# Reciprocal roots with one Newton step and one cubic step in an encoder kernel on Trainium2

## The chip, the cores and the metric

The kernel runs on one core of a Trainium2 chip. Five engines work side by side and wait for one another by semaphores: TensorE (in the profile PE, its weight loads PEld), VectorE (DVE), ScalarE (ACT), GpSimd (POOL) and SyncE (SP), which issues the transfers. The metric is the time of one execution on the device in microseconds.

## The reference

Two transformer blocks of different make stand behind one another. Norms are everywhere in them, and each needs the reciprocal of a square root:

```python
def rms_norm(x, gain=None):
    xf = x.astype(jnp.float32)
    y = xf * lax.rsqrt(jnp.mean(xf * xf, axis=-1, keepdims=True) + EPS)   # EPS = 1e-6
    ...
def _layernorm(x, g, b):
    ...
    y = (xf - mu) * lax.rsqrt(var + LN_EPS) * g.astype(jnp.float32) + b.astype(jnp.float32)
```

In the first block (two layers, on 256 rows of x and 256 rows of the context z, 1024 wide), each of

```python
x = x + 0.5 * mx[2] * swiglu(modulate(rms_norm(x), mx[0], mx[1]), ffn1_w1[l], ffn1_w3[l], ffn1_w2[l])
hx = modulate(rms_norm(x), mx[3], mx[4]) @ w_in[l]
x = x + mx[5] * (mix_x @ w_out[l])
x = x + 0.5 * mx[8] * swiglu(modulate(rms_norm(x), mx[6], mx[7]), ffn2_w1[l], ffn2_w3[l], ffn2_w2[l])
```

has a norm over a row; the heads of the attention branches and of the gated linear attention are normed one by one. The second block (two layers) norms its latents, the heads of a difference attention, and its rows by layer norms.

## The kernel before

TensorE multiplies in float32 by three products (high x high, low x high, high x low; lines L119 to L121). The weights come as chunks of 1 MB in a ring of buffers; ScalarE copies a chunk to its high half (L266, in the second block L2172), VectorE subtracts to get the low half (L277, L2180). The chunks are worked in one long order, and the stages between projections (norms, turns, attention) are woven into it step by step: an engine takes a step of a stage at set places between the groups of its products, so each engine has one fixed queue, and what stands ahead in it delays what follows. Products with the unit matrix (`stream`, L127) fill set numbers of places at which TensorE would wait.

A row norm with its turn is the stage `RmsTurn`. ScalarE squares the rows in four halves and sums each half (L1054 in `Residual`, L1091 in `Squares`) into `row_squares`; VectorE adds the two halves (L1221), applies the mean's factor 1/1024 and epsilon (L1222), takes the reciprocal root (`root_steps`), and writes it on two diagonal matrices (L1225), with which TensorE turns and scales the rows (L1197, 32 rows in the trace). ScalarE and VectorE then apply the modulation (L1142, L1160) and split the result (L1151, L1168). There are 11 such stages.

`root_steps` is used by all norms: for a row norm on a tile 128 x 2, for the norms of heads on 128 x 4 to 128 x 16 (`HeadNorm`, L1762; GpSimd multiplies by its result, L1773), for the latents (`Norms`, L2545), for the heads of the difference branch (`DiffNorm`, L2729; the product L2734 follows) and for the layer norms (`LayerNorm`, L2912; L2918 and ScalarE's L2886 follow). It makes a first guess from the bits (L1239 shifts, L1240 subtracts from a constant) and takes three Newton steps, r <- r (1.5 - 0.5 s r^2), of three operations each (L1242 to L1244). All are on VectorE and each waits for the one before by a semaphore (`link`).

In the profile further names stand: L733 turns the modulation's columns out of PSUM and so frees a bank for L711, the modulation's products; L830 multiplies the gate of a feed-forward network and frees a bank too; L781 makes the low half of that product, for which the next down projection waits in `DownPiece.pe` before its first group and before any step that is woven into it; L2493 finds an attention row's maximum for ScalarE's exponential L2471.

Of the kernel before, what the change touches and what calls it, by code (L numbers as in the profile page):

```python
# [11 lines left out]
ACT = mybir.ActivationFunctionType  # L12
ALU = mybir.AluOpType
# [3 lines left out]
D = 1024  # L17
# [23 lines left out]
EPS = 1e-6  # L41
# [69 lines left out]


ROOT_GUESS = float(0x5F3759DF)
TAB = dict(le=0, gt=1, lt=2, ge=3, ones=4)


# [79 lines left out]
class Woven:  # L196
# [59 lines left out]
    def hi(self, act, m, h, own=False):  # L256

        if m >= len(self.pieces):
            self.follow.hi(act, m - len(self.pieces), h)
            return  # L260
        if not self.pieces[m].parted or (self.pieces[m] in self.own_hi and not own):
            return
        s, r = m % RING, self.half(m, h)
        if h == 0:
            act.wait_ge(self.loaded[s].sem, self.loaded[s].at(m // RING + 1))
        act.activation(self.high[s][:, r], self.raw[s][:, r], ACT.Copy).then_inc(self.highs.sem, 1)  # L266

    def lo(self, dve, m, h, own=False):

        if m >= len(self.pieces):  # L270
            self.follow.lo(dve, m - len(self.pieces), h)
            return
        if not self.pieces[m].parted or (self.pieces[m] in self.own_lo and not own):
            return
        s, r = m % RING, self.half(m, h)
        dve.wait_ge(self.highs.sem, 2 * self.pieces[m].parted_before + h + 1)
        dve.tensor_tensor(self.low[s][:, r], self.raw[s][:, r], self.high[s][:, r].bitcast(F32),  # L277
                          ALU.subtract).then_inc(self.lows.sem, 1)
# [5 lines left out]
    def lo_next(self, dve, m, h):  # L284

        if not self.over_raw(m + 1):
            self.lo(dve, m + 1, h)
# [56 lines left out]
class Piece:  # L344
# [24 lines left out]
    def act(self, act, step):  # L369
        n = self.steps  # L370
        for s in range(n // 2):
            step()
        self.early("act", act)
        self.w.hi(act, self.m + 2, 0)
        for s in range(n // 2, n):
            step()
        self.w.hi(act, self.m + 2, 1)
        self.late("act", act)

    def dve(self, dve, step):  # L380
        n = self.steps
        self.w.lo_next(dve, self.m, 0)
        for s in range(n // 4):
            step()
        self.w.lo_next(dve, self.m, 1)
        for s in range(n // 4, n // 2):
            step()
        self.early("dve", dve)
        for s in range(n // 2, n):
            step()  # L390
        self.w.lo_ahead(dve, self.m)
        self.late("dve", dve)
# [24 lines left out]
class After(Stage):  # L417
# [11 lines left out]
    def pe(self, pe):  # L429
        yield from self.hold("pe")  # L430
# [586 lines left out]
class Residual(Stage):  # L1017
# [32 lines left out]
    def act(self, act):  # L1050
        for b in range(4 if self.ss is not None else 0):
            t, side = b // 2, slice((b % 2) * 512, (b % 2 + 1) * 512)
            act.wait_ge(self.added.sem, self.added.at(b + 1))
            last = act.activation(self.w.ps[:, b, :], self.x[:, t, side], ACT.Square, accum_out=self.ss[:, t, b % 2:b % 2 + 1])  # L1054
        if self.ss is not None:
            last.then_inc(self.squares.sem, 1)
        yield


class Squares(Stage):  # L1060
# [24 lines left out]
    def act(self, act):  # L1085
        self.ready(act)
        if self.side:
            act.wait_ge(self.opened.sem, self.opened.at(1))
        for b in range(4):
            t, side = b // 2, slice((b % 2) * 512, (b % 2 + 1) * 512)  # L1090
            last = act.activation(self.w.ps[:, 4 + b % 2 if self.side else b, :], self.x[:, t, side], ACT.Square,  # L1091
                                  accum_out=self.ss[:, t, b % 2:b % 2 + 1])
            if b < 3:
                self.w.act_link(last)
        last.then_inc(self.squares.sem, 1)
        yield
# [77 lines left out]
class RmsTurn(AffineTurn):  # L1174
# [43 lines left out]
    def dve(self, dve):  # L1218
        b, link = self.b, self.w.dve_link
        self.squares(dve)  # L1220
        link(dve.tensor_tensor(b["var"][:, :], self.ss[:, :, 0], self.ss[:, :, 1], ALU.add))  # L1221
        link(dve.tensor_scalar(b["var"][:, :], b["var"][:, :], 1.0 / D, EPS, ALU.mult, ALU.add))  # L1222
        root_steps(dve, link, b["var"][:, :], b["root"][:, :], b["root_tmp"][:, :])
        for t in range(2):
            dve.tensor_scalar(b["diag"][:, t, :], self.w.eye, b["root"][:, t:t + 1], None, ALU.mult).then_inc(self.scaled.sem, 1)  # L1225
        yield
        yield from [False] * self.lag
        yield from self.held("dve")
        for part in range(2):
            self.mod.wait_part(dve, self.part + part)  # L1230
        if self.room:
            self.room(dve)
        self.dve_turn(dve)
        yield


def root_steps(dve, link, ss, r, t, done=None):

    link(dve.tensor_scalar(t.bitcast(I32), ss.bitcast(I32), 1, None, ALU.arith_shift_right))  # L1239
    link(dve.tensor_scalar(r.bitcast(I32), t.bitcast(I32), -1.0, ROOT_GUESS, ALU.mult, ALU.add))  # L1240
    for i in range(3):
        link(dve.tensor_tensor(t, r, r, ALU.mult))  # L1242
        link(dve.scalar_tensor_tensor(out=t, in0=t, scalar=-0.5, in1=ss, op0=ALU.mult, op1=ALU.mult))
        last = dve.scalar_tensor_tensor(out=r, in0=t, scalar=1.5, in1=r, op0=ALU.add, op1=ALU.mult)  # L1244
        if i < 2 or done is None:
            link(last)
        else:
            last.then_inc(done.sem, 1)


class OutPiece(ProjectionPiece):
# [240 lines left out]
class GlaLevels(Stage):  # L1492
# [29 lines left out]
    def pe(self, pe):  # L1522
        w, f, a, dec = self.w, TAB, self.a, self.dec
        self.ready(pe)
        for kind, m, pair in self.order:
            if kind == "decay":
                w.open(pe, 4)
                for d in range(2):
                    for t in range(2):
                        tab = len(TAB) + d * GLA_LEVELS + m if m < GLA_LEVELS else ((f["gt"], f["le"]), (f["ge"], f["lt"]))[d][t]  # L1530
                        at = (2 * d + t) * P
# [78 lines left out]
class GlaState(Stage):  # L1610
# [13 lines left out]
    def pe(self, pe):  # L1624
        w, f = self.w, TAB
        parts = [[[(0, f["gt"]), (1, f["ones"])], [(1, f["gt"])]], [[(0, f["lt"])], [(1, f["lt"]), (0, f["ones"])]]]
# [88 lines left out]
class HeadNorm(Stage):  # L1715
# [36 lines left out]
    def dve(self, dve):  # L1752
        link, n = self.w.dve_link, self.n
        flat = [self.s[k][:, 0:2 * n] for k in ("ss", "root", "tmp")]
        ss = flat[0].rearrange("p (t h) -> p t h", t=2)
        dve.wait_ge(self.squares.sem, self.squares.at(1))
        for t in range(2):
            last = dve.tensor_reduce(ss[:, t, :], self.junk[:, t, 0:n * HD].rearrange("p (h d) -> p h d", d=HD), AX, ALU.add)
        last.then_inc(self.summed.sem, 1)
        dve.wait_ge(self.summed.sem, self.summed.at(1))  # L1760
        yield
        link(dve.tensor_scalar(flat[0], flat[0], 1.0 / HD, EPS, ALU.mult, ALU.add))  # L1762
        root_steps(dve, link, *flat, done=self.roots)
        yield
# [755 lines left out]
class Norms:  # L2520
# [21 lines left out]
    def dve(self, dve):  # L2542
        m, link = self.mla, self.w.dve_link
        dve.wait_ge(self.squares.sem, self.squares.at(1))
        link(dve.tensor_scalar(m["ss"][:, 0, :], m["ss"][:, 0, :], 1.0 / Q_LORA, EPS, ALU.mult, ALU.add))  # L2545
        link(dve.tensor_scalar(m["ss"][:, 1, :], m["ss"][:, 1, :], 1.0 / KV_LORA, EPS, ALU.mult, ALU.add))
        flat = lambda a: a[:, :, :].rearrange("p a t -> p (a t)")
        root_steps(dve, link, flat(m["ss"]), flat(m["root"]), flat(m["root_tmp"]))
        dve.tensor_copy(m["ss"][:, 0, 0:1], m["root"][:, 0, 0:1]).then_inc(self.roots.sem, 1)
        yield  # L2550
# [1623 lines left out]
```

## Time and profile before

| | us |
|---|---|
| median of 3 runs | 3108.55 |
| lowest, highest | 3102.3, 3112.1 |
| profiled execution | 3110.55 |
| its span, first to last instruction | 3108.8 |
| TensorE busy | 3005.6 (97%) |
| VectorE busy | 1759.8 (57%), 2646 instructions |
| ScalarE busy | 1470.3 (47%), 2182 instructions |
| GpSimd busy | 152.0 (5%) |
| mean granted clock of TensorE | 0.99 of full |

A busy share says how much an engine had to do, not whether anything waited for it. For that there is the chain that ended last, followed back from the last instruction, and for each instruction the time that its engine stood still before it, with what ended that. A timeline merges instructions of one line that follow each other; the "x" is then their number and the duration that of all.

### The profile page before, as it was taken

To read this page: it belongs to the slowest core of one execution; us is meant where nothing else is said; L and a number is where in the kernel's file an instruction comes from. 1 tells how busy PE (TensorE), PEld (TensorE's weight loads), DVE (VectorE), ACT (ScalarE), POOL (GpSimd) and SP (SyncE) were. 2 spreads that over 40 slices of the span, in tenths; PEclk is the share of its full clock that TensorE was granted. 3 is DMA by queue.
4 is the path that set the end of the run, shared out by engine and by line. 5 is a ranking of instruction groups with operands and counts; after the bars stand their busy time and mean duration, and the time that the engine had idled before them with its cause. 6 is when DMAs were issued, how large, how long until landed. Compare 5 with 4: busy or idle time off the path is not lost.

```text
span 3108.8 us, 53689 instructions
## 1 busy us (share of the span) xinstructions
PE 3005.6 (97%) x23104; PEld 2756.7 (89%) x23104; DVE 1759.8 (57%) x2646; ACT 1470.3 (47%) x2182; POOL 152.0 (5%) x147
## 2 busy tenths in 40 slices
PE   8999999999999999999999999999999999999998
PEld 6899788898889998899898889999999999999997
DVE  5445555655546545455646454464756656475665
ACT  4344445453544443444444444455654444565443
POOL 0000000001000000000200000001110101110000
PEclk9999999999999999999999999999999999999999
DMA  7775445664555556765365445554355655445563
GB/s 284 276 236 165 150 163 191 209 197 137 158 192 175 185 186 203 261 217 165 122 181 165 160 157 185 189 177 135 121 161 190 202 190 154 128 122 171 172 198 132
DMA packets 409688, 556.64 MB, mean 179 GB/s; under 512 B 25276, under 2 KB 357996, under 8 KB 409068
## 3 DMA queue, kind: packets, MB, share of 16 engines
q1 hardware_dynamic: 409452, 553.20, 54.5%
q8 instruction: 183, 3.00, 0.4%
q14 instruction: 53, 0.43, 0.0%
HBM read 552.12 MB, written 1.05 MB: 178 GB/s over the span
## 4 chain that ended last, share of the span: by engine, by line
PE 85%; DVE 7%; ACT 3%; DMA 3%; issue 2%; SPq 0%; POOL 0%; DVEq 0%; ACTq 0%
PE psum L119 24%; PE psum L121 24%; PE psum L120 24%; PE psum L711 1%; DMA wr<-in_ffn_w_dram 1%; PE psum L2430 1%; DVE wl L277 1%; PE psum L1922 1%; PE psum L2346 1%; PE psum L2421 1%; DVE wl L2180 1%; PE psum L1545 1%; PE psum L1197 1%; PE psum L1532 1%; PE psum L127 1%
## 5 line engine op out<-in xcount | busy, mean ns | idle before, releaser
L277 DVE TENSOR_TENSOR wl<-wr,wh 128x1024 fp32r<-128x1024 f32 (+1 forms) x558 | 658.9, 1216 | 229.0 <-ACT wh L266 228.2
L266 ACT ACTIVATE wh<-wr 128x1024 fp32r<-128x1024 f32 (+1 forms) x558 | 554.9, 1039 | 231.0 <-DMA wr<-in_ffn_w_dram 208.7
L119 PE MATMUL psum<-xt_hi,wh 128*128 128x256 f32 (+1 forms) x2000 | 566.3, 283 | 3.5 <-DVE wl L277 2.4
L120 PE MATMUL psum<-xt_lo,wh 128*128 128x256 f32 (+1 forms) x2000 | 558.8, 279 | 0.0
L121 PE MATMUL psum<-xt_hi,wl 128*128 128x256 f32 (+1 forms) x2000 | 558.6, 279 | 0.0
L2180 DVE TENSOR_TENSOR wl<-wr,wh 128x1024 fp32r<-128x1024 f32 (+3 forms) x336 | 391.2, 1200 | 121.8 <-ACT wh L2172 120.9
L119 PEld LDWEIGHTS psum<-xt_hi,wh 128*128 128x128 f32 (+1 forms) x2000 | 377.1, 189 | 15.1 <-issue 7.5
L120 PEld LDWEIGHTS psum<-xt_lo,wh 128*128 128x128 f32 (+1 forms) x2000 | 377.2, 189 | 2.3
L121 PEld LDWEIGHTS psum<-xt_hi,wl 128*128 128x128 f32 (+1 forms) x2000 | 378.2, 189 | 0.1
L2172 ACT ACTIVATE wh<-wr 128x1024 fp32r<-128x1024 f32 (+3 forms) x336 | 323.3, 999 | 102.3 <-DMA wr<-in_mlp_w_dram 73.8
L119 PE MATMUL psum<-wh,xt_hi 128*128 128x256 f32 (+1 forms) x1280 | 366.2, 286 | 2.3 <-ACT vv L3337 1.7
L120 PE MATMUL psum<-wl,xt_hi 128*128 128x256 f32 (+1 forms) x1280 | 357.9, 280 | 0.0
L121 PE MATMUL psum<-wh,xt_lo 128*128 128x256 f32 (+1 forms) x1280 | 357.8, 280 | 0.0
L119 PE MATMUL psum<-zt_hi,wh 128*128 128x256 f32 (+1 forms) x1072 | 309.0, 288 | 4.8 <-DVE wl L277 3.6
L120 PE MATMUL psum<-zt_lo,wh 128*128 128x256 f32 (+1 forms) x1072 | 299.6, 279 | 0.0
L121 PE MATMUL psum<-zt_hi,wl 128*128 128x256 f32 (+1 forms) x1072 | 299.4, 279 | 0.0
L119 PE MATMUL psum<-wh,gated_hi 128*128 128x512 f32 x616 | 251.9, 409 | 3.7 <-DVE wl L277 2.2
L119 PEld LDWEIGHTS psum<-wh,xt_hi 128*128 128x128 f32 x1280 | 242.3, 189 | 3.2 <-DVE wl L2180 2.1
L121 PE MATMUL psum<-wh,gated_lo 128*128 128x512 f32 x616 | 243.7, 396 | 0.0
L120 PE MATMUL psum<-wl,gated_hi 128*128 128x512 f32 x616 | 243.6, 395 | 0.0
L120 PEld LDWEIGHTS psum<-wl,xt_hi 128*128 128x128 f32 x1280 | 242.1, 189 | 0.1
L121 PEld LDWEIGHTS psum<-wh,xt_lo 128*128 128x128 f32 x1280 | 241.3, 189 | 0.0
(464 smaller groups left out, 5314.7 us busy)
## 6 DMA issues: line engine op xcount, KB each, us to landing
wr<-in_ffn_w_dram SPq DMA_DIRECT2D x231, 1024.0 KB, 5.4
wr<-in_w_in_dram SPq DMA_DIRECT2D x88, 1024.0 KB, 5.3
wr<-in_w_mod_dram SPq DMA_DIRECT2D x72, 1024.0 KB, 5.1
wr<-in_mlp_w_dram SPq DMA_DIRECT2D x64, 1024.0 KB, 5.2
wr<-in_w_out_dram SPq DMA_DIRECT2D x20, 1024.0 KB, 5.1
wr<-in_mem_w_kv_dram SPq DMA_DIRECT2D x8, 1024.0 KB, 5.0
wr<-in_w_branch_dram SPq DMA_DIRECT2D x16, 512.0 KB, 3.5
wr<-in_w_branch_dram SPq DMA_DIRECT2D x8, 1024.0 KB, 5.0
```

The source lines that it names most:

```text
L119: pe.matmul(out, a[0], b[0], start=first, stop=False)
L120: pe.matmul(out, a[0], b[1], start=False, stop=False)
L121: return pe.matmul(out, a[1], b[0], start=False, stop=last)
L127: pe.matmul(out, eye, eye, start=True, stop=True)
L266: act.activation(self.high[s][:, r], self.raw[s][:, r], ACT.Copy).then_inc(self.highs.sem, 1)
L277: dve.tensor_tensor(self.low[s][:, r], self.raw[s][:, r], self.high[s][:, r].bitcast(F32), ALU.subtract).then_inc(self.lows.sem, 1)
L711: last = pe.matmul(self.group_rows(j), b["silu"][:, at:at + MOD_COLS], cols[:, j], start=(k == 0), stop=(k == 1), tile_position=(0, j * MO ...
L1197: return pe.matmul(out, self.x[:, t, k * P:(k + 1) * P], self.b["diag"][:, t, :], start=True, stop=True)
L1532: last = pe.matmul(w.ps[:, 4, at:at + P], a[:, t, d * P:(d + 1) * P], dec[:, tab, :], start=True, stop=True)
L1545: last = pe.matmul(w.ps[:, 4 + i, pair * 256 + t * P:pair * 256 + (t + 1) * P], src[:, 256 + jt * P:256 + (jt + 1) * P], src[:, it * P:(it ...
L2172: act.activation(self.high[s][:, r], self.raw[s][:, r], ACT.Copy).then_inc(self.highs.sem, 1)
L2180: dve.tensor_tensor(self.low[s][:, r], self.raw[s][:, r], self.high[s][:, r].bitcast(F32), ALU.subtract).then_inc(self.lows.sem, 1)
```

## The change

Root steps: the guess stays. The first Newton step now leaves its result multiplied by 3/8; the second step is of third order: with u = s r^2 (r the unscaled value), r <- r (15 - 10 u + 3 u^2) / 8. Since r' = 3r/8 is what is stored, four operations do it: t = r'^2, t = (64/9) t s (which is u), t = (t - 10/3) t, and r = (t + 5) r'. So nine operations become seven.

Row norms: ScalarE's squares carry a scale of 1/32, so that their sums hold the factor 1/1024 of the mean, and one operation adds the two halves and epsilon, where two stood. The order of the instructions on each engine is otherwise as it was.

```diff
@@ ROOT_GUESS
 ROOT_GUESS = float(0x5F3759DF)
+CUBIC = 3 / 8
@@ Residual.act
-            last = act.activation(self.w.ps[:, b, :], self.x[:, t, side], ACT.Square, accum_out=self.ss[:, t, b % 2:b % 2 + 1])
+            last = act.activation(self.w.ps[:, b, :], self.x[:, t, side], ACT.Square, scale=D ** -0.5,
+                                  accum_out=self.ss[:, t, b % 2:b % 2 + 1])
@@ Squares.act
-            last = act.activation(self.w.ps[:, 4 + b % 2 if self.side else b, :], self.x[:, t, side], ACT.Square,
+            last = act.activation(self.w.ps[:, 4 + b % 2 if self.side else b, :], self.x[:, t, side], ACT.Square, scale=D ** -0.5,
                                   accum_out=self.ss[:, t, b % 2:b % 2 + 1])
@@ RmsTurn.dve
-        link(dve.tensor_tensor(b["var"][:, :], self.ss[:, :, 0], self.ss[:, :, 1], ALU.add))
-        link(dve.tensor_scalar(b["var"][:, :], b["var"][:, :], 1.0 / D, EPS, ALU.mult, ALU.add))
+        link(dve.scalar_tensor_tensor(out=b["var"][:, :], in0=self.ss[:, :, 0], scalar=EPS, in1=self.ss[:, :, 1], op0=ALU.add, op1=ALU.add))
@@ root_steps
-    for i in range(3):
-        link(dve.tensor_tensor(t, r, r, ALU.mult))
-        link(dve.scalar_tensor_tensor(out=t, in0=t, scalar=-0.5, in1=ss, op0=ALU.mult, op1=ALU.mult))
-        last = dve.scalar_tensor_tensor(out=r, in0=t, scalar=1.5, in1=r, op0=ALU.add, op1=ALU.mult)
-        if i < 2 or done is None:
-            link(last)
-        else:
-            last.then_inc(done.sem, 1)
+    square = lambda: link(dve.tensor_tensor(t, r, r, ALU.mult))
+    square()
+    link(dve.scalar_tensor_tensor(out=t, in0=t, scalar=-0.5 * CUBIC, in1=ss, op0=ALU.mult, op1=ALU.mult))
+    link(dve.scalar_tensor_tensor(out=r, in0=t, scalar=1.5 * CUBIC, in1=r, op0=ALU.add, op1=ALU.mult))
+    square()
+    link(dve.scalar_tensor_tensor(out=t, in0=t, scalar=CUBIC ** -2, in1=ss, op0=ALU.mult, op1=ALU.mult))
+    link(dve.scalar_tensor_tensor(out=t, in0=t, scalar=-10 / 3, in1=t, op0=ALU.add, op1=ALU.mult))
+    last = dve.scalar_tensor_tensor(out=r, in0=t, scalar=5.0, in1=r, op0=ALU.add, op1=ALU.mult)
+    if done is None:
+        link(last)
+    else:
+        last.then_inc(done.sem, 1)
```

## Rows read from the trace of the kernel before

**Rows 1.** The page's chain that ended last, share of the span by engine

```profile
PE 85%; DVE 7%; ACT 3%; DMA 3%; issue 2%; SPq 0%; POOL 0%; DVEq 0%; ACTq 0%
```

**Rows 2.** Source view, L1239: count, duration ns min/median/max, first and last start us, forms

```profile
L1239 DVE TENSOR_SCALAR row_small<-row_small x11: 169/170/172, 14.6 to 1836.5; 128x2 int32<-128x2 int32 x11
L1239 DVE TENSOR_SCALAR head_tmp<-head_ss x11: 170/173/176, 337.4 to 1754.9; 128x8 int32<-128x8 int32 x4, 128x16 int32<-128x16 int32 x3, 128x12 int32<-128x12 int32 x3, 128x4 int32<-128x4 int32 x1
L1239 DVE TENSOR_SCALAR ln_tmp<-ln_var x4: 168/169/170, 2377.0 to 3098.3; 128x2 int32<-128x2 int32 x4
L1239 DVE TENSOR_SCALAR latent_tmp<-latent_ss x2: 169/170/171, 2072.3 to 2623.4; 128x4 int32<-128x4 int32 x2
L1239 DVE TENSOR_SCALAR diff_tmp<-diff_ss x2: 175/175/175, 2240.6 to 2784.0; 128x16 int32<-128x16 int32 x2
```

**Rows 3.** VectorE's timeline, row norm at 1189: start us, us, operation, [idle before <-releaser]

```profile
1189.00 0.16 DVE L1221 TENSOR_TENSOR row_small<-row_squares 128x2 f32<-128x2 f32 x1 [0.86 <-ACT psum L1054]
...
1189.80 0.16 DVE L1242 TENSOR_TENSOR row_small<-row_small 128x2 f32<-128x2 f32 x1
...
1191.37 0.16 DVE L1244 SCALAR_TENSOR_TENSOR row_small<-row_small 128x2 f32<-128x2 f32 x1
...
1191.96 0.44 DVE L733 STREAM_TRANSPOSE mod_turned<-psum 128x256 f32<-128x256 f32 x1
```

**Rows 4.** VectorE's timeline, head norm at 337 us, the first and the ninth Newton operation

```profile
337.84 0.17 DVE L1242 TENSOR_TENSOR head_tmp<-roots_na 128x16 f32<-128x16 f32 x1
...
339.51 0.17 DVE L1244 SCALAR_TENSOR_TENSOR roots_na<-head_tmp,roots_na 128x16 f32<-128x16 f32 x1
```

**Rows 5.** TensorE's timeline, work behind a standstill, and one L711 group without

```profile
344.50 2.02 PE L127 MATMUL psum<-eye 128*128 128x128 f32 x10 [3.41 <-DVE gated L830]
...
603.24 2.50 PE L1197 MATMUL psum<-diag,x 128*128 128x128 f32 x20 [0.96 <-DVE wl L277]
...
697.46 3.78 PE L127 MATMUL psum<-eye 128*128 128x128 f32 x16 [3.10 <-DVE gated L830]
...
1187.99 1.07 PE L711 MATMUL psum<-wr,silu_cond 128*32 128x256 f32 x16
1192.55 1.94 PE L711 MATMUL psum<-wr,silu_cond 128*32 128x256 f32 x16 [3.49 <-DVE mod_turned L733]
...
1503.53 2.47 PE L127 MATMUL psum<-eye 128*128 128x128 f32 x20 [1.89 <-issue]
...
1697.96 4.22 PE L1197 MATMUL psum<-diag,x 128*128 128x128 f32 x32 [2.82 <-DVE diag L1225]
...
1759.39 0.44 PE L1430 MATMUL psum<-eye,z_gqa_kv 128*128 128x128 f32 x2 [1.15 <-POOL z_gqa_kv L1777]
...
1839.21 5.87 PE L1197 MATMUL psum<-diag,x 128*128 128x128 f32 x32 [4.88 <-DVE diag L1225]
...
2380.77 1.07 PE L2879 MATMUL psum<-eye,x 128*128 128x128 f32 x8 [0.61 <-ACT x L2886]
...
2790.98 1.16 PE L2421 MATMUL psum<-mem_k,mem_q 128*128 128x256 f32 x4 [1.47 <-ACT probs L2471]
```

**Rows 6.** The chain that ended last, at 1692 and at its end: start us, us, what

```profile
1692.30 5.30 DMA wr<-in_w_in_dram
...
3104.33 1.28 DVE x L2983
```

**Rows 7.** VectorE's timeline at 1502.74

```profile
1502.74 0.68 DVE L781 TENSOR_TENSOR gated_lo<-gated,gated_hi 128x512 fp32r<-128x512 f32 x1
```

**Rows 8.** Source views of ScalarE's L1091 and L1142, columns as in rows 2

```profile
L1091 ACT ACTIVATE psum<-x x20: 601/602/603, 9.1 to 1835.3; 128x512 f32<-128x512 f32 x20
...
L1142 ACT ACTIVATE affine<-psum,mod x44: 543/564/568, 30.3 to 1845.8; 128x256 f32<-128x256 f32 x44
```

**Rows 9.** Windows: us, busy PE, PEld, DVE, ACT, POOL, granted clock, DMA share, GB/s

```profile
1836.00:1838.00 2.00, 0.00 (x0) 0.00 (x0) 1.58 (x10) 2.00 (x4) 0.00 (x0) 0.67 1.10 349
...
1696.00:1698.00 2.00, 0.04 (x1) 0.04 (x1) 1.72 (x11) 0.38 (x1) 0.00 (x0) 1.00 1.08 358
```

## The prediction, made before the changed kernel had run

> **What bounds the kernel now.** I read the chain of waits first: which engine's work, followed back from the last instruction, has no slack. 85% of it is TensorE and 7% VectorE [rows 1]. The change touches VectorE almost alone, so it can only count where VectorE stands in that chain. Next I read the source view of the first instruction of a root, the shift. Its counts say how many roots the program takes: 11 for the row norms (width 2), 11 for the head norms, 4 for the layer norms, 2 latent and 2 of the difference branch, 30 in all [rows 2]. Then the timeline of VectorE around them: a root is a train of small operations, each of which waits for the one before it on its own engine, so it costs its start-to-start step times its length [rows 3, 4]. Last, the timeline of TensorE, for the stretches in which it stood still and what ended them [rows 5]: only roots that such a stretch waits for are worth anything.
>
> **What the change removes.** A row norm's train before its two diagonal matrices is 13 operations now (add, mean and epsilon, shift, guess, three times three) and 10 after: the pair of additions becomes one, nine Newton operations become three and four. The other 19 roots go from nine to seven operations behind the guess. Removed in all: 11 x 3 + 19 x 2 = 71 operations. The step in a row norm is (1189.80 - 1189.00) / 4 = 0.20 us for the first ones and (1191.37 - 1189.80) / 8 = 0.196 us in the Newton part [rows 3]; in a head norm of width 16 it is (339.51 - 337.84) / 8 = 0.209 us [rows 4]. So VectorE does 71 x 0.2 = 14 us less in the whole program. The new operations have forms that the train already holds (one tensor times or plus a constant, times a tensor), so I give them the same step; the one that takes the same tile on both sides, (t - 10/3) t, has no row of its own. Its bounds are a step of 0.196 us, as its neighbours have, and twice that, if the tile had to be read twice over. I take 0.196, since the squaring L1242 reads one tile on both sides already and keeps that step; the other end stands among the rivals.
>
> The Trainium skill (VectorE: DVE Perf Modes, section on the TRN2 errata) says that a small operation pays a fixed cost whatever its width, and, in its rules for kernel authors, that one should reduce the number of operations and not the semaphores between them. By it the price is per operation, as above; steps of 0.196 us at width 2 and 0.209 us at width 16 agree.
>
> **Which of the 30 roots count.** For each I followed the chain of waits through its place.
> - Row norms: 3 of 11 are in the chain, at 597, 1189 and 1836 us. TensorE stands still behind them for 0.96, 3.49 and 4.88 us [rows 5], more than the 3 x 0.196 = 0.59 us that go, so nothing else is late first. 3 x 0.59 = 1.8 us.
> - The row norm at 1695 looks like one of them (2.82 us of standing, ended by the diagonals [rows 5]) and I count it at nothing: the chain goes round it, through a weight transfer issued at 1692.30 that lands 5.30 us later, and ScalarE's copies of it, which hold back the turn that follows [rows 6]. That transfer doesn't start earlier. If the cover is gone, 0.59 us are to be had.
> - Head norms: 7 of 11. Two before 344.50 (TensorE then waits 3.41 us for a product queued behind both on VectorE), one before 697.46 (3.10 us), two before 1503.53 (1.89 us), two before 1759.39 (1.15 us, by way of GpSimd) [rows 5]. The stretch of 1.89 us is put down to nothing by the profile; I count it because it ends 0.11 us behind the subtraction L781, which stands right behind a root on VectorE and on which the down projection's first product waits [rows 7]. 7 x 2 x 0.209 = 2.9 us, each place's share below its stretch.
> - Difference branch: both of 2, through a maximum and an exponential (1.47 us before 2790.98, and a like one of 0.85 us before the other) [rows 5]. 2 x 2 x 0.209 = 0.8 us.
> - Layer norms: all 4; TensorE waits 0.61 us before 2380.77 [rows 5], 0.83 and 0.87 us at the two like places, against 0.39 us that go, and behind the last one there is only VectorE until the end [rows 6]. 4 x 2 x 0.196 = 1.6 us.
> - The other 14 (8 row, 4 head, 2 latent) stand where TensorE is busy or waits for a transfer or ScalarE. Nothing.
>
> Sum on the path: 1.8 + 2.9 + 0.8 + 1.6 = 7.1 us, half of the 14 us. The 16 roots are one behind another in one chain, so the shares add.
>
> **The squares.** The scale in the Square activations changes no count. Such an activation takes 602 ns for 512 columns [rows 8]. The nearest row for a dearer form is L1142, which takes its scale and shift from columns of a tile: 564 ns for 256 columns, where half of 602 would be 301 [rows 8]; not all of that is the operands. Were the scale to cost 0.16 us an activation, the two places where ScalarE's squares are in the chain (one before 1189, four before 1836) would give back 5 x 0.16 = 0.8 us. Lower bound 0. I take 0, since the scale here is a constant in the instruction and the compared form reads two columns. The Trainium skill (ScalarE: Activation LUTs, What ACT_TABLE_LOAD costs) says that an operand read from a column adds to an activation and a constant scale or bias doesn't; no row here shows a Square with a scale.
>
> **The sum.** The profiled execution took 3110.55 us, 1.75 us over its span; 3110.55 - 7.1 = 3103.5. It lies 2.0 us above the median of the runs, 3108.55; from that it is 3101.5. The profiled one holds four falls of the clock that I price next, and looks like one of the dearer executions; I forecast **3101.5 us**.
>
> **Rivals.** *Clock falls that go with the standing.* At 1836 to 1838 us, while TensorE stood, its granted clock went to 0.67 on the mean of 2 us, so to the lower of its two levels (1.2 of 2.4 GHz); at 1696 to 1698, after 2.82 us of standing, it stayed at 1.00 [rows 9]. What a fall costs: the same 32 diagonal products took 5.87 us behind it and 4.22 us without [rows 5], 1.65 us; the 16 products L711 at 1192.55 took 1.94 us against 1.07 us at 1187.99, as at 62 other places. The clock fell at four of the stretches above (3.41, 3.10, 3.49 and 4.88 us) and not at 2.82 or 1.89 us. The change makes these 2.6, 2.7, 2.9 and 4.3 us. If three of the four falls go, at 1.7 to 2.5 us each, another 5 to 7.5 us go: 3094 to 3096.5 us. With one or two gone it is 3097 to 3100. For: the three land at or under a length that was spared. Against: one spared stretch is no rule, and other stretches of 2 to 3 us may take their turn. The Trainium skill (TensorE: Matmul & The Clock Gate, Part 1) says that the chip judges activity on a beat of its own that doesn't start with the kernel; by it a shorter standing makes a fall less likely, without a fixed boundary, and moves it from run to run. It is a reason for a spread of a few us, such as the 3102.3 to 3112.1 of the runs before.
>
> *The gain is taken back by what is late next.* Weight transfers at 1695 already do that. If a transfer or ScalarE's copies were as late at 1189, 1836 and the two attention places (1.8 - 0.6 + 0.8 = 2.0 us) and the stretch put down to nothing isn't ended by L781 (0.8 us), 4.3 us are left: 3104.3 us. The length of the stretches speaks against it.
>
> *The change doesn't do what it says.* If the operation (t - 10/3) t took two steps, the 16 roots of the chain would give back 16 x 0.196 = 3.1 us: 3101.5 + 3.1 = 3104.6 us; with the squares' 0.8 us on top 3105.4 us. If every one of the three or four new forms did, nothing would be left. L1242's rows speak against it.
>
> *Slower.* The clock falls more often: the schedule behind 337 us shifts against the chip's beat, and stretches that were spared (2.82, 1.89, 0.96 us, those of the layer norms) come to fall. At 2.5 us a fall and 7.1 us in hand, three falls more than now bring it to nothing, and from seven more on (7 x 2.5 - 7.1 = 10.4 us) it is slower than 0.3%: about 3119 us. All but the first of the spared stretches get shorter, so this needs ill luck seven times.
>
> **How the numbers follow.** What a measurement of this kernel can tell from no change is about 0.3%, 9.3 us: the bound is 3099.2 us. Forecast case, the sum with at most one fall gone or come (3099 to 3104): 0.50, of which 0.04 below the bound. Falls go with the standing: 0.33, all below it but 0.01. Taken back: 0.10. The new operation dearer: 0.03. Slower case: 0.04, of which 0.03 over +0.3%. So faster 0.36, same 0.61, slower 0.03. The range that leaves out 2 in 10 reaches from most of the clock's gain, 3094, to 3108, where 0.5 us of the sum is left.
>
> **What would show it.** 71 instructions fewer on VectorE (2646 now); the train at the 1189 us place 0.59 us shorter between the first addition and L733; the wait for the diagonals at 1192 near 2.9 and at 1839 near 4.3 us, for L830 near 2.6 and 2.7 us; the same Square at 602 ns; 30 roots, 16 of them in the chain. The clock in the windows at these places decides between the forecast and its neighbour. It would be wrong if a stretch kept its length with a new releaser, or if one of the new operations showed over 200 ns.

## The result: 12 to 13 us faster, of which about 7 are the removed steps

| | before | after |
|---|---|---|
| median of the runs (5 each, side by side), us | 3107.11 | 3094.63 |
| lowest, highest of the new kernel, us | | 3091.26, 3096.9 |
| ratio, 95% interval | | 0.9949, 0.9934 to 0.9964 |
| profiled execution, us (its span) | 3110.55 (3108.8) | 3091.26 (3089.5) |
| TensorE busy, us | 3005.6 | 2990.4 |
| VectorE busy, us (instructions) | 1759.8 (2646) | 1747.1 (2575) |
| mean granted clock, profiled execution | 0.990 | 0.994 |

The forecast was 3101.5 us with 3094 to 3108 around it. The time measured is inside the range, 7 us below the forecast, and faster by more than 0.3%, to which the prediction gave 0.36. Run a second time on another occasion the changed kernel gave 3097.32 us (ratio 0.9962, 0.9948 to 0.9976). The mean of the ten runs is 3096.0 us, against 3109.2 us for the 57 runs of the kernel before that were timed beside the experiments: **13.2 us**, where the sum on the path was 7.1. Taken side by side the means differ by 12.8 and 11.7 us, so the 13.2 is uncertain by about 1 us, and the ratio of 0.9949 in the table lies further from 1 than that of its two medians, 0.9960.

The page of the kernel after: busy time by engine, and the chain that ended last.

```profile
PE 2990.4 (97%) x23104; PEld 2741.7 (89%) x23104; DVE 1747.1 (57%) x2575; ACT 1470.9 (48%) x2182; POOL 151.9 (5%) x147
...
PE 85%; DVE 7%; ACT 3%; DMA 2%; issue 2%; SPq 0%; POOL 0%; DVEq 0%; ACTq 0%
```

71 instructions are gone from VectorE and none from another engine; the bound is the same. TensorE's instructions match one to one, and its busy time fell by 15.2 us although it does the same work. Much of that is chance: in the repeated executions (below) the kernel before has 2997.5 us and the kernel after 2997.2.

Now the row norm of [rows 3] on VectorE after the change: start us, us, operation.

```profile
1181.94 0.16 DVE L1223 SCALAR_TENSOR_TENSOR row_small<-row_squares 128x2 f32<-128x2 f32 x1 [0.86 <-ACT psum L1055]
...
1183.33 0.16 DVE L1247 SCALAR_TENSOR_TENSOR row_small<-row_small 128x2 f32<-128x2 f32 x1
1183.52 0.16 DVE L1248 SCALAR_TENSOR_TENSOR row_small<-row_small 128x2 f32<-128x2 f32 x1
1183.72 0.16 DVE L1249 SCALAR_TENSOR_TENSOR row_small<-row_small 128x2 f32<-128x2 f32 x1
...
1184.31 0.44 DVE L734 STREAM_TRANSPOSE mod_turned<-psum 128x256 f32<-128x256 f32 x1
```

From the first addition to the turn it is 2.37 us, where [rows 3] gave 2.96: 0.59 us less, as predicted. L1248, the operation that takes one tile on both sides, has the step of its neighbours. The Square with its scale costs what the plain one did [rows 8]:

```profile
L1093 ACT ACTIVATE psum<-x x20: 601/602/603, 9.3 to 1822.6; 128x512 f32<-128x512 f32 x20
```

TensorE's timeline of the kernel after, at the places of [rows 5] (in brackets: idle before, and what ended it):

```profile
342.63 1.38 PE L128 MATMUL psum<-eye 128*128 128x128 f32 x10 [2.98 <-DVE gated L831]
...
598.25 2.50 PE L1199 MATMUL psum<-diag,x 128*128 128x128 f32 x20 [0.38 <-DVE wl L278]
...
690.21 2.27 PE L128 MATMUL psum<-eye 128*128 128x128 f32 x18 [2.68 <-DVE gated L831]
...
1184.90 1.94 PE L712 MATMUL psum<-wr,silu_cond 128*32 128x256 f32 x16 [2.90 <-DVE mod_turned L734]
...
1493.36 2.47 PE L128 MATMUL psum<-eye 128*128 128x128 f32 x20 [1.04 <-issue]
...
1748.03 0.44 PE L1435 MATMUL psum<-eye,z_gqa_kv 128*128 128x128 f32 x2 [0.76 <-POOL z_gqa_kv L1782]
...
1825.97 5.49 PE L1199 MATMUL psum<-diag,x 128*128 128x128 f32 x32 [4.29 <-DVE diag L1226]
...
2365.91 1.07 PE L2884 MATMUL psum<-eye,x 128*128 128x128 f32 x8 [0.21 <-ACT x L2891]
...
2772.67 1.16 PE L2426 MATMUL psum<-mem_k,mem_q 128*128 128x256 f32 x4 [1.04 <-ACT probs L2476]
```

Each counted standstill of [rows 5] has shrunk: 3.41 to 2.98, 0.96 to 0.38, 3.10 to 2.68, 3.49 to 2.90, 1.89 to 1.04, 1.15 to 0.76, 4.88 to 4.29, 0.61 to 0.21, 1.47 to 1.04. None kept its length, and none has a new releaser. The amounts are the counted ones but at two places. Of the 0.84 us for two roots at 1759, only 0.39 show there; the rest shows at TensorE's wait 3.8 us ahead of it, 0.91 to 0.50. At 344 only 0.43 of the 0.84 us came. VectorE itself stood still there ahead of the product that TensorE waits for, 0.29 us that the profile puts down to nothing:

```profile
341.43 0.17 DVE L1249 SCALAR_TENSOR_TENSOR roots_gqa<-head_tmp,roots_gqa 128x12 f32<-128x12 f32 x1
341.89 0.69 DVE L831 TENSOR_TENSOR gated<-silu,psum 128x512 f32<-128x512 f32 x1 [0.29 <-issue]
```

The repeated execution shows the same 0.29 us. With the roots changed alone (an experiment below) the stop isn't there and TensorE's wait is 2.63 us, the full amount. What it waits for was not found.

The row norm at 1695, which the prediction counted at nothing, gave nothing. TensorE's way from one L711 group to the stream behind the norm, kernel before and then after:

```profile
1694.07 1.07 PE L711 MATMUL psum<-wr,silu_cond 128*32 128x256 f32 x16
...
1702.02 1.95 PE L127 MATMUL psum<-eye 128*128 128x128 f32 x16
```

```profile
1686.81 2.05 PE L1199 MATMUL psum<-diag,x 128*128 128x128 f32 x16 [2.22 <-DVE diag L1226]
1689.57 2.05 PE L1199 MATMUL psum<-diag,x 128*128 128x128 f32 x16 [0.71 <-ACT affine L1144]
1691.46 1.95 PE L128 MATMUL psum<-eye 128*128 128x128 f32 x16
```

The wait for the diagonals is 0.60 us shorter, and a wait of 0.71 us for ScalarE's modulation is new; from the group (1683.51 in the kernel after) to the stream it is 7.95 us in both.

So the path sum was right but for some 0.4 us, and the question is where the other 5 to 6 us are. Two rows give the first hint: the 10 products behind 342.63 took 1.38 us where [rows 5] had 2.02, and those at 1825.97 took 5.49 against 5.87; at 1184.90 nothing changed.

TensorE's clock, in windows of 20 us: start and end, busy PE, PEld, DVE, ACT, POOL, granted clock, DMA share, GB/s. First the kernel before, then the kernel after.

```profile
340.00:360.00 20.00, 15.37 (x123) 13.08 (x122) 15.01 (x30) 10.71 (x13) 6.18 (x6) 0.91 0.44 150
680.00:700.00 20.00, 16.90 (x124) 14.26 (x123) 10.68 (x29) 11.84 (x15) 3.86 (x2) 0.92 0.48 157
1180.00:1200.00 20.00, 16.51 (x112) 12.47 (x110) 11.48 (x32) 6.72 (x14) 0.00 (x0) 0.83 0.79 262
...
2580.00:2600.00 20.00, 17.79 (x138) 17.29 (x137) 18.68 (x14) 12.35 (x19) 11.82 (x4) 0.91 0.27 77
```

```profile
340.00:360.00 20.00, 15.93 (x131) 13.41 (x132) 13.65 (x26) 10.65 (x12) 4.60 (x5) 1.00 0.38 127
680.00:700.00 20.00, 16.72 (x153) 15.53 (x152) 16.81 (x35) 10.13 (x14) 10.33 (x7) 1.00 0.47 158
1180.00:1200.00 20.00, 13.12 (x104) 9.92 (x97) 13.54 (x34) 11.40 (x18) 0.00 (x0) 0.77 0.83 264
...
2580.00:2600.00 20.00, 20.00 (x177) 19.82 (x177) 13.68 (x12) 10.23 (x15) 5.88 (x8) 1.00 0.62 189
```

Falls to the lower level (1.2 of 2.4 GHz) are gone at 340, at 680 and at 2580, a place where the prediction looked for none; at 1180 the fall has stayed, and a new one stands at 716. Over the whole trace, up to 3060 us, TensorE's clock was at the lower level for 51.2 us before and 30.7 us after. One trace each is not proof: the experiments have to show what of it goes with the change.

### The profile page after: what moved, and what is told of

The parts are those of the page before. It is cut to its first block, busy times and chain, and to the rows that moved or that the text cites. A ratio compares the mean times of both kernels' runs of the same rounds, so it can differ in the third digit from the quotient of the medians.

```text
span 3089.5 us, 53618 instructions
## 1 busy us (share of the span) xinstructions
PE 2990.4 (97%) x23104; PEld 2741.7 (89%) x23104; DVE 1747.1 (57%) x2575; ACT 1470.9 (48%) x2182; POOL 151.9 (5%) x147
## 4 chain that ended last, share of the span: by engine, by line
PE 85%; DVE 7%; ACT 3%; DMA 2%; issue 2%; SPq 0%; POOL 0%; DVEq 0%; ACTq 0%
PE psum L120 24%; PE psum L122 24%; PE psum L121 24%; PE psum L712 2%; DMA wr<-in_ffn_w_dram 1%; PE psum L2435 1%; PE psum L1927 1%; PE psum L2351 1%; PE psum L2426 1%; DVE wl L278 1%; DVE wl L2185 1%; PE psum L1550 1%; PE psum L1199 1%; PE psum L128 1%; PE psum L1537 1%
## 5 line engine op out<-in xcount | busy, mean ns | idle before, releaser
L120 PEld LDWEIGHTS psum<-xt_hi,wh 128*128 128x128 f32 (+1 forms) x2000 | 375.8, 188 | 16.1 <-issue 8.2
```

The source lines that it names most:

```text
L120: pe.matmul(out, a[0], b[0], start=first, stop=False)
```

## The experiments

Theory A: the path sum of 7.1 us, and on top of it TensorE's clock, which falls less where standstills are shorter. Rival B: the roots outside the chain are worth something too (14 us are gone from VectorE, and 13 came). Rival C: the one operation less in the sums, or the scaled squares, bring it. Rival D: the two profiled executions differ by chance. All ratios are against the kernel before on the same chip.

**Noise: the kernel before and the kernel after, each again.**

> The kernel before, unchanged, for a second trace of it. The changed kernel's profile is 19.3 us shorter in its span than that of the kernel before, where 7.1 us were counted in the chain of waits. Set instruction by instruction against each other, the two traces show 8.8 us at places where the clock of TensorE was low in one of them, and about 6 us from a rhythm of the product stream (a product of 256 columns starts every 117.7 ns in some stretches and every 113.4 ns in others). Theory A, the rhythm belongs to the kernel's schedule: this trace shows the slow rhythm again at 260 to 317 and 631 to 678 us, and the ratio is 1.000. Theory B, both are drawn anew in each execution: the slow stretches and the falls of the clock stand elsewhere than in the first trace, and the span moves by up to 5 us. Ratio 1.000 under both.

> The changed kernel, unchanged, for a narrower ratio and a second trace of it. The kernel before repeated gave a second trace whose span is 6.9 us shorter than that of its first, with its clock low for 37.5 us instead of 51.2: so the 19.3 us between the first two traces hold some luck. Theory 'path alone': ratio 0.9977 and a mean granted clock as before (0.990). Theory 'path and clock': ratio 0.995 to 0.996 and a mean clock 0.001 to 0.002 higher than the 0.990 of the kernel before, since what the chain of waits gives (7.1 us) leaves some 7 us that the clock has to supply.

Measured: 0.9997 (0.9987 to 1.0007) and 0.9962 (0.9948 to 0.9976). D is out for the gain: it comes again, 11 to 12 us of it. But much of the 19.3 us between the first two profiled executions was chance. The spans of the second two are 3101.9 and 3095.5 us, 6.4 us apart, both at a mean clock of 0.992: near the path sum alone. The falls do move from one execution to the next. This is the row norm of [rows 5] at 1697.96 (32 products, 4.22 us) in the repeated kernel before:

```profile
1692.41 5.47 PE L1197 MATMUL psum<-diag,x 128*128 128x128 f32 x32 [2.82 <-DVE diag L1225]
```

The same standstill of 2.82 us, and this time the clock fell. So a length that is spared once is not spared always, and the length alone doesn't decide. The Trainium skill (TensorE: Matmul & The Clock Gate, Part 1) says that the chip looks at activity on a beat that doesn't start with the kernel; these two rows agree.

**One part alone.**

```diff
@@ roots only: root_steps as in the change, squares and sums as before
+    square = lambda: link(dve.tensor_tensor(t, r, r, ALU.mult))
...
@@ sums only: squares and sums as in the change, three Newton steps as before
-            last = act.activation(self.w.ps[:, b, :], self.x[:, t, side], ACT.Square, accum_out=self.ss[:, t, b % 2:b % 2 + 1])
+            last = act.activation(self.w.ps[:, b, :], self.x[:, t, side], ACT.Square, scale=D ** -0.5,
...
+        link(dve.scalar_tensor_tensor(out=b["var"][:, :], in0=self.ss[:, :, 0], scalar=EPS, in1=self.ss[:, :, 1], op0=ALU.add, op1=ALU.add))
```

> Only the root steps are changed (nine Newton operations become seven in all 30 roots, 60 operations fewer); the two additions of a row norm and the unscaled squares stay. Theory path: 16 roots in the chain x 2 x 0.2 us = 6.5 us less, ratio 0.9979. Theory path and more: the standing of TensorE gets shorter at all 16 places, so most of the clock's and the rhythm's gain comes too, ratio 0.996 to 0.995.

> Only the row norms' sums are changed: squares with a scale, one addition in place of two operations, 11 operations fewer; the roots keep three Newton steps. Theory path: three places x 0.2 us = 0.6 us less, ratio 0.9998, a Square still at 602 ns. If the scale on the squares cost anything, the Square is longer than 602 ns and the ratio up to 1.0002. If one shift of 0.2 us is enough to draw another rhythm or other falls of the clock, the ratio can lie anywhere between 0.997 and 1.003.

Measured: roots only (60 operations less) 3097.76 us, ratio 0.9964 (0.9951 to 0.9976); sums only (11 less) 3108.95 us, 0.9998 (0.9989 to 1.0007). C is out. The sums are worth 3 x 0.196 = 0.6 us on the path, and the interval can't tell that from nothing.

**In the chain, and not in it.** The change's root steps in the 16 roots that the prediction put in the chain, and then in the other 14 (`CUBIC_AT` holds their numbers in the order in which the roots are issued).

```diff
+    n = ROOTS[0]
+    ROOTS[0] += 1
+    if n in CUBIC_AT:
+        return cubic_steps(dve, link, ss, r, t, done)
```

> Only the 16 roots that the prediction found in the chain of waits get the shorter steps (32 operations fewer), the other 14 and the sums stay as before. If the chain is right, this is all of the gain of the kernel with all 30 roots shortened (ratio 0.9964 there): 0.996 to 0.997, and its clock is higher too. If the extra gain comes from the roots that the prediction left out, it is 0.998 (6.5 us).

> Only the other 14 roots get the shorter steps (28 operations fewer, 5.6 us less on VectorE), those of the chain stay. Theory path: no gain, ratio 1.000 (within 0.001), mean clock as before. If VectorE's load counts off the chain too, up to 0.998.

Measured: the 16 alone 3100.58 us, ratio 0.9968 (0.9956 to 0.9981); the 14 alone 3108.84 us, 0.9998 (0.9987 to 1.0008). B is out: 28 operations outside the chain are worth nothing that shows (the interval leaves room for 4 us at most), and 32 in it are worth 9 to 10 us, though 6.5 were counted. The list of the 16 was right, and the price of one was not. TensorE's waits (us in total, times, longest) with the 16, then with the 14:

```profile
PE psum L130 <- DVE gated L833: 5.3, 2, 2.7
...
PE psum L130 <- issue: 1.1, 1, 1.1
```

```profile
PE psum L130 <- DVE gated L833: 6.6, 2, 3.5
...
PE psum L130 <- issue: 1.9, 1, 1.9
```

The stretch that the profile puts down to nothing (1.89 us in [rows 5]) goes with the roots of the chain: 1.1 us with them, 1.9 without.

One place speaks against a simple tie of length and clock. At 344 the roots alone make the standstill 2.63 us, shorter than the 2.98 us of the kernel after, and yet the clock fell behind it and the next 8 products took 1.92 us against 1.06. The roots alone, then the kernel after:

```profile
344.94 1.48 PE L128 MATMUL psum<-eye 128*128 128x128 f32 x10 [2.63 <-DVE gated L831]
346.22 1.92 PE L1537 MATMUL psum<-dec,log_decay 128*128 128x128 f32 x8
```

```profile
343.85 1.06 PE L1537 MATMUL psum<-dec,log_decay 128*128 128x128 f32 x8
```

With the 16 alone it fell there too, behind 2.63 us; in both executions of the kernel after it did not.

**The dose.** The third Newton step left out of all 30 roots, so that they come out rougher (90 operations less, 48 of them in the chain), and a fourth one added (90 more, with `range(4)` in the same line). In both the test for the last step moves along.

```diff
-    for i in range(3):
+    for i in range(2):
```

> The third Newton step is left out of all 30 roots (nine operations become six, 90 fewer; the result is less exact), the rest as before. Theory path: 16 x 3 x 0.2 = 9.7 us less, ratio 0.9969. Theory path and more: as the changed kernel or better, ratio 0.995 to 0.993.

> A fourth Newton step in all 30 roots (90 operations more), otherwise the kernel before. Theory 'path alone': 16 x 3 x 0.2 = 9.7 us more, ratio 1.003. Theory 'path and clock': the standing of TensorE gets longer by 0.6 us at each place, falls of the clock get likelier, mean clock under 0.990 and the ratio 1.004 to 1.007.

Measured: two steps 3093.22 us, ratio 0.9954 (0.9941 to 0.9966); four steps 3124.69 us, 1.0050 (1.0036 to 1.0064). In means that is -14.6 and +15.1 us, where 48 x 0.2 = 9.7 us were counted either way. So the measured price is about 0.31 us for each operation in the chain, one and a half times its step, and it is so in both directions. The waits for L127 with four steps:

```profile
PE psum L127 <- DVE gated L830: 8.4, 2, 4.7
...
PE psum L127 <- issue: 3.1, 1, 3.1
```

The waits themselves grow by the counted amount (1.9 to 3.1 us for six steps of 0.209). So the surplus has to lie in TensorE's work and not in its waits.

**Where the surplus lies.** TensorE's instructions are the same in all kernels above, so the starts can be compared one by one. (Where the line between a step and a wait is drawn moves a whole column by some us; the differences between its rows move by about 1 us.) Three things differ: what TensorE stood still (steps over 0.35 us), what steps at the lower clock took more than the same steps at the full clock elsewhere, and what steps of about the length of a product of 256 columns, at full clock and with no wait between, took over 113.4 ns (below). Sums in us, of one trace each, with the mean clock and mean time of all timed runs of the kernel:

| kernel | standing | low clock | products over 113.4 ns | mean clock | mean time, us |
|---|---|---|---|---|---|
| before | 151.8 | 16.1 | 28.9 | 0.9902 | 3109.2 |
| before again | 151.6 | 11.6 | 26.4 | 0.9905 | 3109.0 |
| sums only | 149.9 | 22.4 | 28.9 | 0.9898 | 3109.6 |
| the other 14 | 150.8 | 11.1 | 26.5 | 0.9902 | 3107.9 |
| roots only | 145.2 | 15.2 | 24.0 | 0.9922 | 3097.8 |
| the 16 | 145.4 | 16.3 | 26.6 | 0.9921 | 3100.3 |
| after | 146.6 | 8.6 | 22.5 | 0.9924 | 3094.3 |
| after again | 143.3 | 12.2 | 27.6 | 0.9918 | 3097.7 |
| two Newton steps | 142.7 | 16.8 | 25.6 | 0.9918 | 3094.6 |
| four Newton steps | 159.8 | 18.0 | 30.0 | 0.9880 | 3124.3 |

Standing falls in two groups, 151.0 us in the first four rows and 145.1 in the next four: 5.9 us, near the 6.7 that the path sum has on TensorE (0.4 of the 7.1 lies behind its last product). Of a single trace the low clock tells little, 11 to 22 us in the same group. The group means are 15.3 and 13.1 us, and the clock was at the lower level for 47.8 us a trace in the first group and 41.0 in the second: less, by about 2 us of time, which the spread doesn't set apart from nothing. The mean clock of all timed runs tells more: 0.9902 in the first group, 0.9918 to 0.9924 in the second, 0.9880 with four steps. Its price is estimated from two sources. Among the 141 timed executions with a clock on record, each compared with the others of its own kernel, the time falls by 2.2 us (standard error 0.2) for 0.001 more of clock. And in the profiled kernel before, 51.2 us at half clock cost 16.1 us; 0.001 of clock is 0.001 x 3109 / 0.5 = 6.2 us at the lower level, or 2.0 us. By these, 0.0019 of clock is worth 3.8 to 4.2 us, if the clock that a change brings is worth as much as the clock that chance brings. Path 7.1 and clock 4 make 11 of the 13.2 us. For four steps: 9.7 and 0.0022 x 2.2 = 4.8 make 14.5 of 15.1; for two: 9.7 and 3.5 make 13.2 of 14.6.

**The clock alone.** If clock is worth 2.2 us a thousandth, filling standstills without shortening them should show it. The kernel before, with 11, 9 and 11 products with the unit matrix behind the squares at the row norms at 1189, 1695 and 1836 us, and the kernel after with 9, 7 and 9. (One product stands as two in the trace: x22 for 11.)

```diff
+    def warm_up(self, pe, at):
+        if at in self.warm:
+            self.squares(pe)
+            stream(pe, self.w.ps[:, 0, 0:P], self.w.eye, self.warm[at])
...
+    x_t7.warm, z_t9.warm, x_t9.warm = {1: 11}, {3: 9}, {3: 11}
```

> The kernel before with nothing changed on VectorE or ScalarE; TensorE gets 11, 9 and 11 products with the unit matrix (0.235 us each) in three of its standstills behind a row norm's root (1189, 1695 and 1836 us), placed between the squares' end and the wait for the diagonals, so that they end before that wait does. Theory clock: the time follows the granted clock, 2.2 us for each 0.001 of its mean (110 timed runs so far); the falls at 1188 and 1833 and that at 1693 us, some 13 us of low clock in an execution, go; mean clock 0.992, ratio 0.998 to 0.999. Theory 'path alone, the rest is something else': the standing ends when it did, so the time stays, ratio 1.000, or gets longer where the products delay what follows.

> The changed kernel with the same filling of three standstills (9, 7 and 9 products, since the standing is 0.6 us shorter). Theory clock: the gain of the filling comes on top where falls are left (the two traces of the changed kernel still show 3.4 to 6.8 us at 1184 and 3.4 us at 1826): mean clock 0.993 to 0.994, ratio 0.993 to 0.995 against the kernel before. Otherwise 0.9955, as the changed kernel's two measurements.

Measured on the kernel before: the mean clock rose from 0.9902 to 0.9928, more than the change itself brought, but the time only to 3105.76 us, ratio 0.9993 (0.9984 to 1.0002); in means 2.5 us beside the kernel before on the same chip and 3.9 against the 57 runs, where 5.7 would answer to the clock. The interval holds 1, so no gain in time is shown, and the 0.998 to 0.999 expected from the clock did not come. Clock gained in this way is worth 1.0 to 1.5 us for 0.001, not 2.2; at that price the change's 0.0019 would be 2 to 3 us and not 4. On the kernel after: clock 0.9932, 3095.17 us, ratio 0.9957 (0.9944 to 0.9969), 1.1 us under the mean of the ten runs of after, which is noise. The fall did go; granted clock 1192 to 1194 us (columns as above), kernel before and then with the filling:

```profile
1192.00:1194.00 2.00, 1.45 (x16) 0.69 (x16) 1.21 (x5) 0.00 (x0) 0.00 (x0) 0.50 1.10 354
```

```profile
1192.00:1194.00 2.00, 1.35 (x19) 0.85 (x20) 1.31 (x5) 0.00 (x0) 0.00 (x0) 1.00 1.10 361
```

TensorE's timeline there, kernel before and with the filling:

```profile
1192.55 1.94 PE L711 MATMUL psum<-wr,silu_cond 128*32 128x256 f32 x16 [3.49 <-DVE mod_turned L733]
1194.42 5.72 PE L1197 MATMUL psum<-diag,x 128*128 128x128 f32 x32
...
1203.43 0.71 PE L127 MATMUL psum<-eye 128*128 128x128 f32 x4 [2.29 <-DVE mod_turned L733]
```

```profile
1188.09 1.07 PE L711 MATMUL psum<-wr,silu_cond 128*32 128x256 f32 x16
1189.09 2.72 PE L127 MATMUL psum<-eye 128*128 128x128 f32 x22
1192.65 1.07 PE L711 MATMUL psum<-wr,silu_cond 128*32 128x256 f32 x16 [0.85 <-DVE mod_turned L733]
1193.65 2.05 PE L1198 MATMUL psum<-diag,x 128*128 128x128 f32 x16
1196.60 2.05 PE L1198 MATMUL psum<-diag,x 128*128 128x128 f32 x16 [0.90 <-ACT affine L1142]
1198.59 1.07 PE L711 MATMUL psum<-wr,silu_cond 128*32 128x256 f32 x16
1202.29 1.22 PE L127 MATMUL psum<-eye 128*128 128x128 f32 x4 [2.63 <-DVE mod_turned L733]
```

The products L711 and L1197 took 7.66 us before and 1.07 + 2.05 + 2.05 = 5.2 with the filling. Of these 2.5 us TensorE now waits 0.90 us for ScalarE's modulation, and 2.63 instead of 2.29 at the end. From the L711 group ahead of the standstill to the stream behind it the way is 1203.43 - 1187.99 = 15.44 us before and 1202.29 - 1188.09 = 14.20 with the filling: 1.2 us, half of the 2.5. At this row norm other engines are late next when TensorE is quick. So a fall there costs 1.2 us and not the 1.7 to 2.5 of the prediction. The norm at 1695 says the same: the way that took 7.95 us without a fall took 9.19 in the repeated kernel before with one, 1.24 us more. What a fall costs in a stream of projections, where the other engines are ahead, was not tried apart.

## Why the prediction was wrong, point by point

- **Path sum, 7.1 us: right but for 0.4.** The train is 0.59 us shorter as named, the standstills at 1184 and 1826 are 2.90 and 4.29 us against 2.9 and 4.3, and that at 690 is 2.68 against 2.7. The one at 342 is 2.98 us against 2.6: with VectorE's stop ahead of L831 something else was late first there. The row norm at 1695 gave nothing, as counted. Roots outside the chain are worth nothing that shows (0.9998).
- **L781 and the stretch without a releaser: right.** It is 1.89 us with three Newton steps, 1.04 with one and the cubic one, 1.1 with the 16 alone and 3.1 with four Newton steps: it follows the number of steps on VectorE.
- **New operations at one step each, squares at 602 ns: right.** Both bounds for dearer forms fell away. No row stands behind the 0.16 us that the prediction set for a dearer scale; it measured 0.
- **Taken back, dearer, slower: none came.** Both measurements of the kernel after lie 0.4 to 0.5% under the kernel before.
- **The step that failed** stands in the rivals and in "How the numbers follow": *forecast case, the sum with at most one fall gone or come, 0.50*, against *clock falls that go with the standing, 0.33*. Having found four falls behind the very stretches that get shorter, I let the path sum alone be the forecast and put the clock's term in it at nothing, as if falls stayed where they were. The runs show that the clock goes with the standing in the mean of many executions: clock 0.9902 to 0.992 with less standing, 0.9880 with more, 0.9902 and 0.9898 where the path is left alone. Worth 4 us by its tie to the time among executions, and 2 to 3 by the filling, it should have been a term of the sum. The sum then gives 3109.2 - 7.1 - 4 = 3098 us, or 3099 to 3100 by the lower price. That the steps on the path bring more than their own length is shown (48 more cost 15.1 us, 48 fewer bring 14.6, with 9.7 counted); that the clock is what brings it is shown in part only.
- **The argument against it was the wrong one.** "One spared stretch is no rule" is true: that stretch of 2.82 us fell in the next execution. But if one length is now spared and now not, falls can go without a boundary being crossed, and that speaks for an expected gain in the sum, not against it. Place by place length doesn't foretell a fall (at 344 the clock fell behind 2.63 us and not behind 2.98); only the mean over many executions goes with it.
- **Within the rival, the size.** Its 3094 to 3096.5 us held the 3094.63, but with three falls at 1.7 to 2.5 us. What came is less clock (2 to 4 us instead of 5 to 7.5), and not three of the four falls: in both executions of the kernel after, the one at 344 is gone and those at 1184 and 1826 stayed. The one at 690 is gone in the first and back in the second, and so is the one at 2580. Some 2 to 4 us more lie elsewhere, as the last section tells. That 3094.63 lies within 3094 to 3096.5 is in part luck.
- **The profiled execution** was called one of the dearer ones and set 2 us above the median. Against the mean of the 57 runs, 3109.2 us, it was 1.4 us above.

## What to carry to other kernels

Count only the steps that a standstill of the busiest engine waits for, and trust such a list: a count along the chain was right at all but one place, and 28 operations outside it were worth nothing that shows. Where that engine is TensorE and standstills of 2 to 5 us are among them, put a term on top of the sum: here each us taken from the chain brought half as much again or more, and each us added cost half as much again. Filling three standstills with products raised the clock more than shortening them did, and saved less: at the place looked at, other engines were late next.

## What the runs showed of the hardware that was not expected

**Two paces of the same stream.** With the clock at 1.00 and no wait, products of 256 columns start about every 113.4 ns or every 117.7 ns, for tens of us at a time. The same instructions in the kernel before and in the kernel after (12 steps in 1.41 us and in 1.36 us):

```profile
305.78 0.28 PE L120 MATMUL psum<-wl,zt_hi 128*128 128x256 f32 x1
...
307.19 0.28 PE L120 MATMUL psum<-wl,zt_hi 128*128 128x256 f32 x1
```

```profile
305.83 0.28 PE L121 MATMUL psum<-wl,zt_hi 128*128 128x256 f32 x1
...
307.19 0.28 PE L121 MATMUL psum<-wl,zt_hi 128*128 128x256 f32 x1
```

The windows show it as a count, 70 and 73 products in 8 us, all of it busy and at full clock in both:

```profile
300.00:308.00 8.00, 8.00 (x70) 8.00 (x69) 2.85 (x4) 2.99 (x6) 0.00 (x0) 1.00 0.31 71
```

```profile
300.00:308.00 8.00, 8.00 (x73) 8.00 (x73) 2.85 (x4) 2.27 (x5) 0.00 (x0) 1.00 0.39 119
```

Of some 17,500 steps of 105 to 125 ns in each trace, 7612 took 116 ns or more in the kernel before, 6777 in its repetition, 6083 in the kernel after and 7265 in its repetition. Part of the stretches is the same in each execution of a kernel and part is not. In the table the first four rows have 27.7 us of it on the mean and the next four 25.2; the difference of 2.5 us is of the size of what path and clock leave open, but its error is over 1 us, and what sets the pace was not found. So of 13.2 us about 7 are shown place by place, 2 to 4 go with the clock by the estimates above, and the last 2 to 4 stay open.
